# Four quadrants for the small products of an RWKV-7 phase, transposes by transpose mode, and output weights staged in halves

## The reference

```python
h = rms_norm(x, norm_pre)
p = h @ w_in                                   # 1024 -> all columns of both groups
# GLA group, 4 heads: S_t = diag(a_t) S_{t-1} + k_t v_t^T,  o_t = q_t S_t
# RWKV-7 group, 8 heads of 64:
prev = concat(s_shift, p_shift[:-1]);  xm = p_shift + mu * (prev - p_shift)
r, kr, vr, wd, ad = split(xm)
w = exp(-0.606531 * sigmoid(w0 + tanh(wd) @ w_up));  a = sigmoid(a0 + ad @ a_up)
kk = kr * k_k;  kr = kr * (1 + (a - 1) * k_a);  kk = kk / |kk| of each head
def step(s, (r_t, w_t, k_t, v_t, kk_t, a_t)):
    sa = s @ -kk_t
    s = s * w_t + sa (kk_t * a_t)^T + v_t k_t^T
    y = s @ r_t
y = group_norm(y) * ln_w + ln_b;  bonus = sum(r * kr * r_k) * vr, per head
o_rwkv = (y + bonus) * silu(z_r)
m = concat(o_gla, o_rwkv) @ w_out
x = x + rms_norm(m, norm_post)
```

## Time and profile before

| | us |
|---|---|
| median of 3 runs (2612.58 to 2613.16) | 2613.08 |
| the profiled execution | 2613.44 |
| its span | 2611.7 |
| first phase, 0 to | 998.56 |
| opening of the second phase (block 0, and pieces for blocks 1 and 2), to | 1179.58 |
| bodies 1 to 14, to | 2162.45 |
| body 15, to | 2243.49 |
| body 16, to | 2309.00 |
| output units alone, to | 2611.70 |

### The profile page before, as it was taken

The page is one execution under the profiler, slowest core; times in us unless marked ns, Lnnn a source line. Parts: engine busy times, 40 slices in busy tenths (PEclk is TensorE's granted clock), DMA queues, the critical chain, the costliest instruction groups (busy, mean ns, idle before and its releaser), DMA issues.

```text
span 2611.7 us, 70434 instructions
## 1 busy us (share of the span) xinstructions
PE 2480.8 (95%) x30628; PEld 1891.0 (72%) x30628; DVE 1295.8 (50%) x2646; ACT 1330.2 (51%) x2368; POOL 623.7 (24%) x1104
## 2 busy tenths in 40 slices
PE   4899999999999995979999999999999997899998
PEld 4677777777777775768888888888888885544443
DVE  4333344433333324456667666776776765442222
ACT  6345566556555544335555555555555553343332
POOL 0000000000000001245555555555555554100000
PEclk9799999999999997989999999999999997999999
DMA  4112222122111112102122212222122214245444
GB/s 188 57 56 76 75 71 66 62 74 89 60 58 53 41 41 76 47 16 72 59 67 67 67 55 67 67 67 59 49 64 56 61 51 146 82 143 159 152 145 137
DMA packets 171027, 202.47 MB, mean 78 GB/s; under 512 B 90080, under 2 KB 125216, under 8 KB 166368
## 3 DMA queue, kind: packets, MB, share of 16 engines
q1 hardware_dynamic: 166352, 180.66, 22.2%
q10 hardware_dynamic: 4368, 17.30, 1.9%
HBM read 117.65 MB, written 80.28 MB: 76 GB/s over the span
## 4 chain that ended last, share of the span: by engine, by line
PE 47%; DVE 4%; POOL 4%; ACT 2%; DMA 2%; issue 1%; SPq 1%; DVEq 0%; POOLq 0%
PE r_d L1616 30%; POOL r_inv L1559 2%; POOL r_inv_tmp L1557 2%; PE r_d L1671 2%; PE r_RZ L1790 2%; PE r_A L1695 1%; PE r_RZ L1765 1%; PE r_A L1719 1%; PE r_d L1643 1%; PE r_d L1660 1%; PE r_RZ L1779 1%; PE r_RY L1803 1%; PE r_d L1817 1%; PE r_RY L1749 1%; PE r_B L1736 1%
## 5 line engine op out<-in xcount | busy, mean ns | idle before, releaser
L1616 PE MATMUL r_d<-r_hT,w_hi 128*128 128x256 f16 (+1 forms) x3536 | 583.4, 272 | 15.2 <-DMA r_hT<-scratch_hT 15.2
L567 PE MATMUL d<-hT,w_hi 128*128 128x256 f16 (+1 forms) x3264 | 525.9, 270 | 1.4 <-DVE hT L840 1.4
L1616 PE MATMUL r_d<-r_hT,w_lo 128*128 128x256 f16 (+1 forms) x1768 | 475.6, 272 | 0.0
L567 PE MATMUL d<-hT,w_lo 128*128 128x256 f16 (+1 forms) x1632 | 436.6, 270 | 0.0
L1616 PEld LDWEIGHTS r_d<-r_hT,w_hi 128*128 128x128 f16 x3536 | 336.7, 99 | 82.4 <-issue 24.3
L567 PEld LDWEIGHTS d<-hT,w_hi 128*128 128x128 f16 x3264 | 315.6, 98 | 51.1 <-issue 12.5
L1557 POOL TENSOR_TENSOR r_inv_tmp<-r_inv 64x30 f32<-64x30 f32 (+14 forms) x480 | 251.6, 524 | 290.5 <-DMA r_inv<-scratch_blocks 254.1
L1616 PE MATMUL r_d<-w_hi,r_ops 128*128 128x512 f16 x1056 | 317.4, 381 | 2.1 <-DVE w_lo L2286 1.7
L1559 POOL TENSOR_TENSOR r_inv<-r_inv,r_inv_tmp 64x30 f32<-64x30 f32 (+14 forms) x480 | 268.9, 560 | 37.6
L1506 POOL MEMSET r_run_s<- 128x128 f16 x1 | 0.2, 205 | 1000.9 <-POOLq L266 1000.9
L1882 ACT ACTIVATE r_praw<-r_d,r_sc 128x256 f32<-128x256 f32 (+1 forms) x221 | 92.5, 467 | 240.9 <-PE r_d L1616 240.8
(11 more groups left out here) (270 smaller groups left out, 4737.6 us busy)
## 6 DMA issues: line engine op xcount, KB each, us to landing
x_tok<-in_x SPq DMA_DIRECT2D x33, 512.0 KB, 4.3
r_ops<-in_x SPq DMA_DIRECT2D x33, 512.0 KB, 4.2
out_y<-r_ops SPq DMA_DIRECT2D x33, 512.0 KB, 2.9
scratch_hT<-hT SPq DMA_DIRECT2D x16, 1024.0 KB, 6.8
r_hT<-scratch_hT ACTq DMA_DIRECT2D x16, 1024.0 KB, 4.8
scratch_mg<-m_hl SPq DMA_DIRECT2D x33, 256.0 KB, 2.0
r_zr<-scratch_zr SPq DMA_DIRECT2D x33, 256.0 KB, 3.3
r_bon<-scratch_bonus SPq DMA_DIRECT2D x33, 256.0 KB, 3.9
```

What stands on the lines that cost most here:

```text
L567: mm = pe.matmul(out, lhs(k, a, w), rhs(k, a, w), start=(n == 0), stop=(n == len(terms) - 1))
L1616: mm = pe.matmul(out, lhs(k, a, w), rhs(k, a, w), start=(m == 0), stop=(m == 3 * KT - 1))
```

## The change

It has five parts.

1. First phase: x is scaled by ScalarE (`scaled_x`) before it is turned, `diag` is gone, and the turn is a PE transpose against the identity.
2. Second phase: the six two-quadrant products, the head sums and `centre` (each cut in 64x64 blocks) take all four quadrants. For that the halves of odd groups are swapped: `swapped(h, g)` is the half that head h of group g has in v, in the unknowns, in y. The four PSUM banks A, B, RZ, RY become two pairs, AB and EO. VectorE writes v (x8, x10) of odd groups in two ops of 64 rows, ScalarE the squares likewise; the centred values take four ScalarE ops of 256 columns and not two of 512.
3. The 32x32 product w becomes `inner`, 64x32, placed ahead of `unknowns` (which is of the chunk before it). It reads the inverse from its own copy T1, sent by four more transfers, and `td` is a job of its own. The state's product for y moves from `meet` into `advance`. `advance` now also waits for `keep_w` of the next chunk, `keep_w` for both copies of the unknowns of the chunk before, `next` for y.
4. The orders are written anew; `xs` and `strict` stand at the end of the body before.
5. The output weights come as 16 pieces of 128x512, column half 0 first, into the columns that each round x6 and x2 of the last projection leaves free, so the first units have room in body 15's x4 and x6: 108 rooms in the last bodies, before 90.

```diff
+def swapped(h, g):
+    return h ^ (g & 1)
...
-                pe.wait_ge(diag_ok.sem, diag_ok.at(tile, 1))
+                pe.wait_ge(scaled_ok.sem, scaled_ok.at(tile, 1))
...
-                    mm = pe.matmul(tr_bank[half][:, k * P:(k + 1) * P],
-                                   x_tok[:, tile % 2, (4 * half + k) * P:(4 * half + k + 1) * P], diag[:, tile % 2, :],
-                                   start=True, stop=True)
+                    mm = pe.transpose(tr_bank[half][:, k * P:(k + 1) * P],
+                                      x_tok[:, tile % 2, (4 * half + k) * P:(4 * half + k + 1) * P], ident[:, :])
...
+                act.activation(x_tok[:, tile % 2, :], x_tok[:, tile % 2, :], ACT.Identity,
+                               scale=s[:, 2:3]).then_inc(*scaled_ok.up(tile))
...
-                        mm = pe.matmul(bA[hrows(h), g * CH:(g + 1) * CH], sxq[hrows(1 - h), s, h, g, 0:CH],
-                                       bu[hrows(1 - h), s, h, 1, g, :], start=True, stop=True)
+                        k = swapped(h, g)
+                        mm = pe.matmul(AB[hrows(k), g % 2, (g // 2) * CH:(g // 2 + 1) * CH],
+                                       sxq[hrows(1 - h), s, h, g, 0:CH], bu[hrows(1 - h), s, k, 1, g, :],
+                                       start=True, stop=True)
...
-                        mm = pe.matmul(bB[r0 + 32:r0 + 64, g * 32:(g + 1) * 32], sxq[r0:r0 + 32, s, h, g, 32:64],
-                                       TD[r0:r0 + 32, ch, g, :], start=True, stop=True, tile_position=(r0, r0 + 32))
+                        mm = pe.matmul(EO[hrows(swapped(h, g)), h, c0:c0 + 32], sxq[hrows(h), s, h, g, 0:CH],
+                                       TD[hrows(h), ch, g, :], start=True, stop=True)
...
-                            mm = pe.matmul(half((RZ, RY)[j // 2], j % 2)[rows, g, :], ops[rows, b % 3, A_, g, cols],
-                                           src, start=True, stop=True)
+                            mm = pe.matmul(EO[hrows(swapped(h, g)), g % 2, c0:c0 + CH],
+                                           ops[hrows(h), b % 3, A_, g, cols], src, start=True, stop=True)
...
-                pe.matmul(out[:, :], centre[:, :], yT[:, tile % 2], start=True, stop=True).then_inc(*d_full.up(m))
+                        mm = pe.matmul(out[hrows(h), (g // 2) * P:(g // 2 + 1) * P], centre[rows, rows],
+                                       yT[rows, tile % 2, g, :], start=True, stop=True)
...
+                if q + 1 < NQ:
+                    pe.wait_ge(w_ok.sem, w_ok.at(q + 1, 1))
...
+                if q:
+                    dve.wait_ge(u_full.sem, u_full.at(q - 1, 1))
+                    dve.wait_ge(uo_ok.sem, uo_ok.at(q - 1, 1))
-                dve.tensor_copy(Wt[:, :, :], bB[:, 0:128].rearrange("p (g t) -> p g t", g=4)).then_inc(*w_ok.up(q))
+                dve.tensor_copy(Wt[:, :, :, :], pairs(EO, 384, 32)).then_inc(*w_ok.up(q))
```

More of the change, by code:

```diff
@@ L979 @@
 PE_BODY = """
[L980 to L983, removed]
+    meet:0 scores:1 centre:0 x12*3 -bs x4 inner:1 unknowns:0 turn:1 x4 out x4*2 advance:0 solve:1 join:1 x4*2
@@ L984 @@
+    variance:0 meet:1 scores:2 out lwa0 x6*4 inner:2 unknowns:1 turn:2 x6 out x6 lwa2 advance:1 solve:2 join:2
+    x0*4 meet:2 out scores:3 x0*2 kn x2*2 inner:3 unknowns:2 turn:3 x2 out x2*2 advance:2 solve:3 join:3 x2
+    centre:1 x8*2 meet:3 out scores:4 x8*4 xs inner:4 unknowns:3 turn:4 variance:1 out x10*2 advance:3 solve:4
+    join:4 x10*4 out
 """.split()
 ACT_BODY = """
-    -deviation:1 taken:x12 -high:1 odd:0 tanh_w out turned:1 z1:1 keep_y:0 join_e:1 taken:x4 out centred:0
-    squares:0 odd:1 turned:2 out taken:x6 deviation:0 z1:2 keep_y:1 join_e:2 tanh:lw0 tanh:la0 out squares:2
@@ L990 @@
+    taken:x2 centred:1 out taken:x8 odd:3 turned:4 out deviation:1 z1:4 join_e:4 keep_y:3 out
 """.split()
 DVE_BODY = """
-    -mixed:x10 -normed:1 masked:1 zc:0 -gated:1 mixed:x12 even:0 -strict:0 out -strict:1 -low:1 keep_w:1 next:0
-    join_o:1 -bonus:0 mixed:x4 out zc:1 -bonus:2 masked:2 even:1 out mixed:x6 keep_w:2 normed:0 next:1 join_o:2
-    gated:0 out zc:2 low:0 masked:3 mixed:x0 decay out even:2 keep_w:3 next:2 join_o:3 clamp:0 mixed:x2 clamp:2
-    out zc:3 k_factor masked:4 unit:0 unit:2 k_prime even:3 mixed:x8 out beta a keep_w:4 next:3 join_o:4 rkk out
+    -gated:1 -mixed:x10 masked:1 zc:0 mixed:x12 -low:1 even:0 out -bonus:0 -bonus:1 keep_w:1 next:0 join_o:1
@@ L996 @@
+    mixed:x4 out masked:2 zc:1 normed:0 gated:0 out even:1 keep_w:2 low:0 mixed:x6 next:1 join_o:2 decay out
+    masked:3 zc:2 clamp:0 clamp:1 k_factor even:2 mixed:x0 out keep_w:3 unit:0 unit:1 next:2 k_prime join_o:3
+    mixed:x2 out beta a masked:4 -td zc:3 mixed:x8 out even:3 keep_w:4 strict:0 strict:1 normed:1 next:3
+    join_o:4 rkk out
 """.split()
@@ L1004 @@
 STEP = ("meet", "unknowns", "advance", "zc", "even", "next", "odd", "keep_y")
-AHEAD = ("scores", "turn", "solve", "join", "masked", "keep_w", "join_o", "turned", "z1", "join_e")
+AHEAD = ("scores", "inner", "turn", "solve", "join", "masked", "keep_w", "join_o", "turned", "z1", "join_e")
 POST = ("centre", "variance", "centred", "deviation", "high", "normed", "gated", "low", "get_gate", "put_m")
 OUT_FROM = LAST - 1
+OW_FROM = -6
+OW_AT = [0, 0, 1, 1, 2, 2, 3, 3, 4, 4, 4, 5, 5, 5, 6, 6]
 def script_jobs(name, arg, b, n):
@@ new lines, in claim_pair, with products @@
+            def claim_pair(key):
+                return [claim(key + (k,)) if key[0] == "centre" else claim((key[0], key[1] + str(k)))
+                        for k in range(2)]
+            def products(b):
+                parts = claim_pair((b, "xs"))
+                pe.wait_ge(op_ok.sem, op_ok.at(b, 2))
+                for ch in range(nchunks(b)):
+                    cols = slice(ch * CH, (ch + 1) * CH)
+                    for g in range(4):
+                        out, m = parts[g % 2]
+                        c0 = (2 * ch + g // 2) * CH
+                        for h in range(2):
+                            mm = pe.matmul(out[hrows(swapped(h, g)), c0:c0 + CH], ops[hrows(h), b % 3, T_, g, cols],
+                                           ops[hrows(h), b % 3, A_, g, cols], start=True, stop=True)
+                        if ch == nchunks(b) - 1 and g >= 2:
+                            mm.then_inc(*d_full.up(m))
```

459 lines of the change are left out of this document (259 added, 200 removed).

## The result

The changed kernel takes 2490.26 us (median of 4 runs, 2485.12 to 2493.19), the one before 2612.83 on the same chip: a ratio of 0.953, 95% interval 0.9513 to 0.9546. It is faster, by 122.6 us where 176 were forecast. The profiled execution took 2489.47 us with a span of 2487.3. The first view is again the windows by stage; with the columns of the earlier trace rows; bodies begin at `meet:0`, which is now L1825.

What follows compares the result with a forecast made beforehand. TensorE's work was taken to bound the bodies. From 2613.44 us, −29.6 + 2 − 3 − 103.6 + 2 − 21.2 − 23.3 = −176.7 gave 2437; own range 2425 to 2447, 8 in 10 for 2405 to 2485.

Steps and rivals of the forecast that it cites:

- Quadrants: Bodies: 64x64 products on four quadrants, not two, save 8.3 us of TensorE's work a body, from 70.2 to 62.1.
- The rule of the Trainium skill on one PSUM bank: Different row tiles can't access one PSUM bank simultaneously; by it two quadrants gain nothing. Given only a small chance.
- Transposes: First phase: one pass of 0.112 us per turn product in place of two, saving 29.6 us over 66 halves.
- the 44.4: First phase: upper bound in us of the transposes' saving, if a transpose takes half of the 0.112.
- Opening: Stage between first phase and bodies: small products saved, more half ops in block 0; −3 us, between −8 and +3.
- Body 16 and tail: Last stages: −15.6 for units moved earlier, −5.2 for small products, −2.5 for half the idle time; −23.3 us.
- The wait of 0.7 us a body: TensorE's waits in each steady body under the new order, raising 62.1 to 62.8 us.
- the round trip: From `strict` to `td`, the inverse's transfers and GpSimd steps, 54.8 us, plus 5.0 on VectorE: no body under 59.8.
- Body 14: Ten of the 16 output weight splits fall here, about 0.7 us each on VectorE: +2 us (0 to 5).
- Rival B: VectorE and the inverse's round trip bound the body: bodies of 64 to 66 us, 2454 to 2482 in all; chance 0.22.
- Rival F: Slower: short waits in each chunk bring TensorE to its 1.2 GHz level, bodies of 80.7 us, 2687; chance 0.04.
- Body 15 at 59.8: Work of 55 us with 36 output units lies below the inverse's round trip, so 59.8; 21.2 saved from 81.04.

Runs made afterwards that it cites:

- experiment 2: The changed kernel with GpSimd's two wide products done on only a few columns, so results are not the layer's: 2439.81 us.
- experiment 4: The changed kernel with the first phase's turns by a diagonal matrix again, as before the change: 2518.64 us.
- experiment 6: The changed kernel with GpSimd's two wide products each in four pieces, and VectorE's mixing of x10 put ahead of the gating: 2446.75 us.
- the first two of 10 to 12: Against experiment 6's kernel, the output weights staged one place earlier, or all sixteen splits ahead of body 15: 2445.75 and 2446.68 us.
- The quarters alone: The changed kernel with GpSimd's two wide products of a block each done in four pieces of 128x256, VectorE's order kept: 2448.3 us.
- experiment 8: The changed kernel in its new order with nothing swapped, so the 64x64 products use two quadrants: 2582.78 us, median of three.

## Why the prediction was wrong, point by point

- **Quadrants: right.** The body's work was put at 62.1. It is 62.6 where nothing waits (experiment 2), and the same order on two quadrants has 7.8 more. The rule of the Trainium skill on one PSUM bank (TensorEngine Tiling (Array Packing), Restrictions and Gotchas), weighed in the prediction, doesn't hold in this kernel: a group of 16 passes sends both row halves to each of two banks and takes 0.26 to 0.28 us, where two in a step would take 0.46.
- **Transposes: right**, one pass each: 26.8 us measured (experiment 4), 27.6 forecast with the start; not the 44.4 that the prediction set beside it. **Opening**: 6.6 saved, 3 forecast, and the size is uncertain: counted from the first phase's last products (971.11 in the trace after) it takes 174.7 us, and 169.6 to 174.8 in the traces of the other kernels here with this same opening. **Body 16 and tail**: 25.8 saved, 23.3 forecast.
- **The wait of 0.7 us a body: wrong, and nearly the whole miss.** It stood for "an order written anew", with 0 and the round trip as its bounds. The step that failed is the pricing of VectorE in the new order: its operations were priced by their usual durations, and the new neighbours were never held against GpSimd's. The gating was moved behind `rkk`, which is what starts GpSimd's wide products, and two operations of 0.9 us together took 4.9. TensorE pays 2.75 us a body, some 0.2 more in `scores`, and about 0.8 on average in clock (1.5 in every second body): 62.6 + 3.75 = 66.35, measured 66.4 in bodies 2 to 13. Body 14 was put at 64.8 and takes 69.1: beside the same 2.75 it waits 1.9 for `keep_w` and 1.0 for `zc`. With GpSimd's products cut short the same order gives 2439.8, 3 us from the forecast. That its bodies 1 to 14 then take 880.6 us, forecast 881.2, bears the account out; that the whole comes so near is in part luck, for its body 15 is 11.1 us too long and the stages on either side 7.2 too short.
- **Rival B** had VectorE late, but for its own load and the inverse's round trip. `td` never waited in 750 us, and the times given for it, up to 2482, end under the result. Its bound, like the range, came from the wrong mechanism.
- **Rival F**, waits that lower the clock, was priced as all or nothing. It happened in small: 1.2 us in every second body, and behind one long wait, not short ones in each chunk.
- **Body 15 at 59.8: wrong by 10.1 us.** The work (58.47 busy at a clock of 0.93, 54 to 55 at full) was right, the bound was not. It was taken to be the round trip alone, but at its start there are no x12 pieces, so `bs` meets three splits, the port and x10 on VectorE with nothing to cover them, 7.4 us:

```profile
2084.17 1.99 PE L1715 MATMUL r_d<-r_scr,r_headsum 64*64 64x256 f32 x16 [7.40 <-issue]
2075.03 1.89 DVE L2390 SCALAR_TENSOR_TENSOR w_lo<-r_hT,w_hi 128x512 f16<-128x512 f32 x3
2075.19 4.52 POOL L1604 TENSOR_TENSOR r_ops<-r_ops,r_gin 128x1024 f32<-128x1024 f32 x1 [24.92 <-DVE r_scr L2240]
```

GpSimd's first product lasts 4.52 us beside the three splits. The gating's second product and the small copy behind them take 2.71 and 2.14, and VectorE's last operation on x10 ends at 2084.07, just ahead of `bs`. The profile names no releaser for this wait, so that it is x10 is read from the times. Which order would bring the body to 60 stays open: each rearrangement tried brought another wait to the front.

The fastest kernels here that compute all of it are that of experiment 6 and the first two of 10 to 12, at 2446 to 2447: 44 us under the changed kernel. The quarters alone, eight short operations for two, give 42 of them.

## What to carry to other kernels

When an order is changed, list for each operation of VectorE with two SBUF inputs, or that copies within SBUF, what GpSimd runs at that moment, and find what releases GpSimd; the signal that starts a long GpSimd operation is the worst neighbour such an operation can have. If they must meet, cut the GpSimd operation in pieces: the wait here was then for one piece. And a forecast that calls the waits of a rewritten order a small constant has a bound of the wrong kind: follow the ring of banks from each claim back to the operation that frees it, once for each body.

## What was not expected of the hardware

- A copy of two columns, 0.16 us alone, took 2.14 beside a GpSimd product of 128x1024 (2.6 us) and 0.69 beside quarters of it.
- VectorE operations with one input in PSUM kept their 0.5 us (128x256) beside the same product.
- One wait of 2.75 us was followed in some bodies by a granted clock of 0.69 to 0.80 over 6.7 us, 1.5 us more of TensorE's time; with waits of 2.0 us one body of twelve was longer than the others, with 1.72 us (experiment 8) none.
- Sixteen passes with 32 moving columns and 64 stationary on four quadrants (`inner`, L1770) take 0.21 to 0.26 us at the full clock, as those with 64 moving columns do (0.25 to 0.28). The prediction had priced them so.
